# A recurrent layer's low-rank products, key norms and decays moved under its projections, 64-row logits and another order at the entrance

## The reference, cut to what matters

```python
# the indexer and the attention of layer 1
rel = relu(einsum('bthd,bsd->bths', qi_blk, ki)); score = einsum('bths,bth->bts', rel, wi_blk)
_, sel = lax.top_k(score, 64)
logits = einsum('btngd,btknd->btngk', qg, k_sel) * HEAD_DIM ** -0.5      # 64 numbers per head
# the recurrent layer
xx = token_shift(h) - h
xs = h[None] + xx[None] * mu[:, None, None, :]                            # six mixes
r, k, v = einsum('cbld,cde->cble', xs[:3], w_rkv)                         # three 1024x1024 projections
xw, xa, xg = xs[3], xs[4], xs[5]
w_log = -softplus(-(w0 + tanh(xw @ w1) @ w2)) - 0.5;  decay = exp(-exp(w_log))
a = sigmoid(a0 + (xa @ a1) @ a2)
g = sigmoid(xg @ g1) @ g2
kk = (k * k_k); kk = kk * rsqrt(max(sum(kk * kk, per head), 1e-24))
k = k * (1 + (a - 1) * k_a)
state = state * w_t + sa * b_t + v_t * k_t                                # b = kk * a, over 256 steps
y = state @ r_t
```

## Time and profile before

| | us |
|---|---|
| median of three runs | 1173.62 |
| profiled execution | 1176.45 |
| its span (first to last instruction) | 1174.8 |
| PE busy in the span | 1109.6 (94%) |
| DVE, ACT, POOL busy | 822.5, 639.3, 227.5 |
| mean granted PE clock | 0.967 of full speed |

### The profile page before, as it was taken

How to read it: one execution, slowest core, us unless ns; L and a number is a source line. 1 busy time by engine, 2 the same in 40 slices (tenths; PEclk the granted TensorE clock), 3 DMA queues, 4 the chain that set the end, 5 groups by cost and what they waited for, 6 DMA issues and landing times.

```text
span 1174.8 us, 23469 instructions
## 1 busy us (share of the span) xinstructions
PE 1109.6 (94%) x9384; PEld 997.0 (85%) x9384; DVE 822.5 (70%) x1103; ACT 639.3 (54%) x949; POOL 227.5 (19%) x171
## 2 busy tenths in 40 slices
PE   6889999999989999998699999989999999999887
PEld 5786798899879868998598899879997999998675
DVE  4687457767769669675767767775766877774774
ACT  4766356565646466324365565644534666664552
POOL 1000033344500005944023344510000000000000
PEclk9998999999999997999799999989999999999989
DMA  7522287877735520000467877746654655656200
GB/s 271 189 73 73 88 270 232 278 249 247 266 110 180 181 58 3 4 3 3 133 228 246 274 251 247 265 125 200 191 163 147 198 191 166 205 172 201 66 1 36
DMA packets 82138, 190.47 MB, mean 162 GB/s; under 512 B 5840, under 2 KB 6112, under 8 KB 81936
## 3 DMA queue, kind: packets, MB, share of 16 engines
q1 hardware_dynamic: 73184, 157.31, 41.4%
q0 software_dynamic: 7584, 27.53, 8.1%
q10 hardware_dynamic: 1296, 4.58, 1.0%
HBM read 188.34 MB, written 1.05 MB: 161 GB/s over the span
## 4 chain that ended last, share of the span: by engine, by line
PE 75%; DVE 11%; ACT 4%; DMA 4%; issue 3%; POOL 2%; ACTq 0%; DVEq 0%; POOLq 0%; SPq 0%
PE bank L1944 12%; PE bank L1945 12%; PE bank L1946 12%; PE bank L1920 4%; PE bank L1922 4%; PE bank L1921 4%; PE bank L2159 4%; PE bank L2160 4%; PE bank L2161 4%; PE bank L2335 3%; DVE w_lo L1185 2%; DMA mod_w<-in_w_mod_dram 2%; POOL mod_all L510 1%; PE bank L2231 1%; PE bank L2447 1%
## 5 line engine op out<-in xcount | busy, mean ns | idle before, releaser
L1185 DVE TENSOR_TENSOR w_lo<-raw,w_hi 128x1024 fp32r<-128x1024 f32 x296 | 390.4, 1338 | 211.4 <-ACT w_hi L652 211.2
L652 ACT ACTIVATE w_hi<-raw 128x1024 fp32r<-128x1024 f32 x296 | 310.2, 1056 | 296.9 <-PE bank L1946 149.3
L1944 PE MATMUL bank<-act_hi,w_hi 128*128 128x256 f32 x1392 | 390.2, 280 | 1.4 <-DVE act_lo L1227 0.8
L1945 PE MATMUL bank<-act_lo,w_hi 128*128 128x256 f32 x1392 | 390.1, 280 | 0.0
L1946 PE MATMUL bank<-act_hi,w_lo 128*128 128x256 f32 x1392 | 389.6, 280 | 0.0
L1944 PEld LDWEIGHTS bank<-act_hi,w_hi 128*128 128x128 f32 x1392 | 262.4, 189 | 4.2 <-issue 2.8
L1945 PEld LDWEIGHTS bank<-act_lo,w_hi 128*128 128x128 f32 x1392 | 262.3, 188 | 0.9 <-issue 0.2
L1946 PEld LDWEIGHTS bank<-act_hi,w_lo 128*128 128x128 f32 x1392 | 262.4, 188 | 0.0
L510 POOL TENSOR_TENSOR mod_all<-mod_all,mod_w 128x1024 f32<-128x1024 f32 x42 | 109.9, 2617 | 143.3 <-ACT mod_w L829 142.4
L2159 PE MATMUL bank<-w_hi,ff_hi 128*128 128x512 f32 x256 | 103.1, 403 | 8.2 <-DVE ff_lo L1424 8.2
L2160 PE MATMUL bank<-w_lo,ff_hi 128*128 128x512 f32 x256 | 103.3, 403 | 0.0
(11 more groups left out here) (315 smaller groups left out, 1484.2 us busy)
## 6 DMA issues: line engine op xcount, KB each, us to landing
raw<-in_mlp_w_up_dram SPq DMA_DIRECT2D x64, 512.0 KB, 4.9
raw<-in_mlp_w_down_dram SPq DMA_DIRECT2D x64, 512.0 KB, 4.4
raw<-in_dil_w_in_dram SPq DMA_DIRECT2D x64, 512.0 KB, 4.1
mod_w<-in_w_mod_dram POOLq DMA_DIRECT2D x48, 512.0 KB, 4.3
raw<-in_conv_w_in_dram SPq DMA_DIRECT2D x32, 512.0 KB, 4.3
raw<-in_rwkv_w_rkv_dram SPq DMA_DIRECT2D x24, 512.0 KB, 4.7
raw<-in_dsa_w_in_dram SPq DMA_DIRECT2D x16, 512.0 KB, 4.8
raw<-in_dsa_w_o_dram SPq DMA_DIRECT2D x8, 512.0 KB, 3.7
```

The source lines that it names most:

```text
L652: act.activation(w_hi[:, slot, :], raw[:, slot, :], ACT.Copy).then_inc(hi_ready, 1)
L1185: dve.tensor_tensor(w_lo[:, slot, :], raw[:, slot, :], w_hi[:, slot, :].bitcast(F32), ALU.subtract).then_inc(lo_ready, 1)
L1944: pe.matmul(dst, w_hi[:, slot, at], hi[:, kt, :], start=begin, stop=False, skip_group_check=True)
L1945: pe.matmul(dst, w_hi[:, slot, at], lo[:, kt, :], start=False, stop=False, skip_group_check=True)
```

## The change

Recurrent layer. The blocks come in the order keys, receptances, values. The mixes of decay and rate are made before block 2 into buffers of their own, and their first products run together after block 1, one in array columns 0 to 63 and the other in 64 to 127 of the same bank. The gate's first product, the head sums and half of the second products run after block 3, the other half after block 4. Roots are by one POOL instruction on 256 columns (`pow`) instead of ACT's square root, with its table loads, and DVE's reciprocal. Sigmoids, decay sums, exponentials and `ka` move between the splits of blocks 4 and 5. After the last block PE has `spread` and the gate's second product; the turned values move between the scan's first steps of u = 0 and u = 1. POOL makes its half of `k` and `b` only after both early operands. g2 is loaded after the gate's first product.

Layer 1. The indexer and attention logits use 64 array rows each, heads alternating between rows 0 to 63 and 64 to 127 and between two banks; `kiT`, the zeros of both and the copy on ACT are gone. The ReLU of the first four steps comes before `rope_bank(3, 2)`. ACT rounds the first activations after two granules, not four. The constants that layer 1 does not need, the norm row and the gate rows are loaded by ACT just before the attention units.

```diff
 # POOL
-            key_zeros()
-                pool.wait_ge(granule_used, STREAM["rwkv_out"])            # load_g2
+                pool.wait_ge(lora_full, 2)
             def rwkv():
                 load_g2()
+                pool.wait_ge(sums_ready, 1)
+                pool.tensor_tensor(per_head[:, :], per_head[:, :], half_neg[:, 0:1].broadcast_to([P, SEQ]), ALU.pow).then_inc(kk_inverse, 1)
+                pool.wait_ge(operands, 2)
                 pool.wait_ge(ka_ready, 2)
 # ACT, layer 1
-                split_block(base, 0)
+                for q in range(2): split_hi(base, q)
                 round_f(0)
+                for q in range(2, PER_BLOCK): split_hi(base, q)
...
-                for half in range(2): mv = act.activation(S["kiT"][rows, half, :], S["ki_rot"][rows, :], ACT.Copy)
                 split_block(base, 8)
+                for n in range(4): relu_scores(n)
                 act.wait_ge(granule_used, base + 8)
                 rope_bank(3, 2)
...
                 rope_bank(6, 6)
+                late_loads()                                              # five DMA issues
 # ACT, recurrent layer
+                splits(4, 8); leave(0); splits(8, 11); round_mix(1, (0, 1)); splits(11, 12); round_mix(1, (2, 3)); leave(1)
+                (tanh and copy of R["mid"] from bank[4])
+                splits(12, 13); round_mix(2, (0, 1)); splits(13, 14); round_mix(2, (2, 3)); splits(14, 16); leave(2)
+                splits(16, 18); (square of raw_kk); splits(18, 20); leave(3); (sigmoid of gmid)
+                open_gates(0); keep_a(0); splits(20, 24); leave(4)
+                open_gates(1); keep_a(1); decays(0); leave(5); decays(1)
 # DVE, recurrent layer
-                split_block(base, 4); mix(1); rest_mix(1); split_block(base, 8); mix(2); rest_mix(2); ...
+                splits(4, 6); mix_part(1, 0, 1); splits(6, 7); mix_part(1, 2, 3); splits(7, 8)
+                mix_part(2, 0, 1, 2, 3); mix_part(3, 0, 1); splits(8, 9); rest_part(1, 0); mix_part(3, 2); rest_part(1, 1)
+                splits(9, 10); mix_part(3, 3); rest_part(1, 2, 3); splits(10, 11); mix_part(4, 0, 1); splits(11, 12)
+                mix_part(4, 2, 3); splits(12, 13); rest_part(2, 0, 1, 2, 3); splits(13, 14); (raw_kk); splits(14, 15)
+                mix_part(5, 0, 1); splits(15, 16); mix_part(5, 2, 3); splits(16, 20)
+                dve.wait_ge(kk_sums, 1)
+                dve.tensor_scalar(per_head[:, :], bank[1][:, 0:SEQ], 1e-24, None, ALU.max).then_inc(sums_ready, 1)
+                sum_decays(0); splits(20, 22)
+                dve.tensor_tensor(R["k"][:, at, :], R["k"][:, at, :], R["ka"][:, at, :], ALU.mult).then_inc(k_early, 1)
+                splits(22, 24); sum_decays(1); means(0)
 # PE, recurrent layer, after block n
+                    if n == 1: lora_decay_and_rate()
-                        lora(0, ((0, LORA),))
+                    if n == 3: lora_gate(); head_sums(1, R["kk_square"]).then_inc(kk_sums, 1); second_lora(0)
-                        lora(1, ((0, LORA),))
+                    if n == 4: second_lora(1)
-                lora(2, ((0, GHALF), (GHALF, GHALF)))
 # PE, rwkv_mid
+                pe.wait_ge(kk_inverse, 1)
+                pe.wait_ge(lora2_ready, 8)
+                spread(4).then_inc(kk_spread, 1)
...
 # PE, scan_loop, first turn
                             pe.wait_ge(operands, u + 1)
-                            pe.wait_ge(*((vT_ready, 4) if u == 0 else (glora_ready, 4)))
+                            if u: turn_values()
+                            pe.wait_ge(*((glora_ready, 4) if u == 0 else (vT_ready, 4)))
 # PE, logits
+                    for e in range(2): (mask product into bank[2 * slot + e])
                     for j in range(2):
-                        mm = pe.matmul(dst, S["qT"][:, 2 * n + j, i * P:(i + 1) * P], S["kT"][:, n, :, 0:w], ...)
+                        for e in range(2):
+                            rows = slice(e * HD, (e + 1) * HD)
+                            mm = pe.matmul(bank[2 * slot + e][:, j * w:(j + 1) * w], S["qT"][rows, 2 * n + j, i * P:(i + 1) * P],
+                                           S["kT"][rows, n, 0:w], start=False, stop=True, skip_group_check=True)
```

More of the change, by code:

```diff
@@ L732, in dsa, with relu_scores @@
                 rope_bank(2, 1)
[L734 to L745, removed]
+                def relu_scores(n):
                     act.wait_ge(idx_full, n // 2 + 1)
@@ L898, in rwkv_in, with splits, keep_a @@
                     round_mix(0, (b,))
-                split_block(base, 4)
-                round_mix(1)
+                def splits(first, last):
+                    for k in range(first, last):
+                        split_hi(base, k)
+                def keep_a(half):
+                    act.wait_ge(less_ready, 1)
+                    act.wait_ge(kk_sums, 1)
+                    act.wait_ge(lora2_ready, 4 * half + 4)
+                    for pair in range(4 * half, 4 * half + 4):
+                        kept = act.activation(R["ka"][:, pair, :], mixer["a"][:, pair, :], ACT.Identity, bias=less_k_a[:, pair:pair + 1], scale=K_A[:, pair:pair + 1])
+                    kept.then_inc(ka_ready, 1)
@@ new lines, in open_gates @@
+                def open_gates(half):
+                    for pair in range(4 * half, 4 * half + 4):
+                        act.wait_ge(lora2_full, 2 * (pair // 2) + 2)
+                        src = slice(pair % 2 * SEQ, (pair % 2 + 1) * SEQ)
+                        for j, (bias, dst) in enumerate(((W0, less), (A0, mixer["a"]))):
+                            sg = act.activation(dst[:, pair, :], bank[4 + 2 * (pair % 4 // 2) + j][:, src], ACT.Sigmoid, bias=bias[:, pair:pair + 1])
+                        sg.then_inc(lora2_ready, 1)
@@ new lines, in second_lora @@
+                def second_lora(half):
+                    if half == 0:
+                        pe.wait_ge(mid_ready, 2)
+                    else:
+                        pe.wait_ge(lora2_ready, 4)
+                    for pair in range(4 * half, 4 * half + 4):
+                        for j, rows in enumerate((slice(0, LORA), slice(LORA, P))):
+                            mm = pe.matmul(bank[4 + 2 * (pair % 4 // 2) + j][:, pair % 2 * SEQ:(pair % 2 + 1) * SEQ], R["w2a2"][rows, pair * P:(pair + 1) * P],
+                                           R["mid"][rows, :], start=True, stop=True)
+                        mm.then_inc(lora2_full, 1)
@@ L2308, in rwkv_mid @@
                                 at = (j * CHUNKS + c) * CHUNK
-                                mm = pe.matmul(bank[b][rows, at:at + CHUNK], R["uv"][values, 2 * b + j, c, h, :], unit[values, :], start=True, stop=True)
+                                mm = pe.matmul(bank[4 + b][rows, at:at + CHUNK], R["uv"][values, 2 * b + j, c, h, :], unit[values, :], start=True, stop=True)
                     mm.then_inc(vT_full, 1)
```

398 lines of the change are left out of this document (220 added, 178 removed).

## The result

The changed kernel is slower: median 1181.25 us over 13 runs (1175.55 to 1186.01) against 1174.95 us of the kernel before, run beside it (1169.27 to 1179.35). The ratio is 1.0059, 95% interval 1.0041 to 1.0078. The forecast, 1168.7, named the wrong sign; its range, 1154 to 1188, holds the time. The profiled execution took 1179.7 us, with a span of 1178.0.

A forecast was written before the change was run, and what follows sets the result against it. PE, busy 94% of the span, was taken as the bound, with most time behind the recurrent layer's last block. 1176.45 - 11.7 + 11.6 - 4.8 = 1171.5 profiled, 2.83 above the median, so 1168.7; range 1154 to 1188.

The forecast's parts named there:

- the root: Recurrent layer: POOL's `pow` on 256 columns takes 19.4 us; 9.6 moves PE, plus 2 for lower clock, 11.6 lost.
- cover: Before the recurrent layer's last block: with DVE held, the root is hidden up to 9.8 us; each us above moves PE.
- (D): Recurrent layer: root long but DVE runs, PE idles 12 us at `spread`; time 1168 to 1177, near 1173; chance 0.11.
- (C): Recurrent layer, gap before block 5: DVE stands still, root 38 us; time 1187.6, range 1177 to 1191; chance 0.24.
- Up to the last block's end: Recurrent layer: 15.5 us of products inside the blocks for 7.3, so the last block ends 8.2 us later, at 433.2.
- DVE's pace: Recurrent layer, blocks 1 to 4: DVE's 35 us of work fits in 37; nothing charged, 3 us kept for the range.
- Behind the last block: Recurrent layer: first scan product at 442.0 instead of 460.4, u = 1 12.9 us earlier; gain 11.7, 8 to 13.
- The collision of POOL's products: Behind the last block: three DVE operands took 2.3 to 2.8 us beside POOL's products; POOL's added wait removes this.
- Layer 1: Attention units and block 12: halved logits gain 4.3 us, the block's end 0.5; gain 4.8 in all.
- or the clock drops: Layer 1's attention units: a case for the low end of their gain, 1 us of a range 1 to 5.
- Block 12: Layer 1: the block ends at 80.4 to 81.3 instead of 82.0, a gain of 0.5 us, 0 to 1.6.

The follow-up runs named there:

- root_act: The changed kernel with the root made by ACT (Sqrt) and DVE (reciprocal) in place of POOL's `pow`: 1162.18 us, ratio 0.9897 to the kernel before.
- rec_only: The kernel before with the recurrent part alone, the root on ACT and DVE, layer 1 as before: 1164.66 us, ratio 0.9905.
- after: The changed kernel itself, with POOL's `pow` and both parts of the change, against the kernel before: 1181.25 us, ratio 1.0059.
- l1_only: The kernel before with the layer-1 part alone, the recurrent layer as before: 1171.67 us, ratio 0.9965.
- the two halves: The kernel before with only the 64-row products and ReLU order, ratio 1.0005, or only the first splits' order and late loads, ratio 0.9991.

## Why the prediction was wrong, point by point

**The step that failed is the root**, in both of its halves. The term was 19.4 us and the row is 41.16; and the text charged it through DVE standing still, cover 9.8, where DVE ran and the cover was some 26 us (404.45 to the last block's end at 430.4). What happened is rival (D), which got 0.11: PE waits at `spread` until 445 (445.67), idle 12 us (15.2), the gate's second product at the lower clock (14.0), first scan product at 455 to 460 (462.5), u = 1 not before 464 (473.9). (D)'s price was too low. It said that the recurrent layer then gains nothing; in truth the layer loses 10.7 us (228.1 against 217.4). The root was 3.2 us longer than the 38 that (D) had, and the lower clock lasted to 468 and not only through the gate's product. The rest was in (D)'s own rows: from 445, `spread` and 13.6 us for the gate's product give 460 for the first scan product, and the 10 us from there to u = 1's end, which the forecast has (442.0 to 452.0), give 470 where the kernel before had 464.9. The range of 1154 to 1188 holds the time by luck: 1181.25 is above (D)'s own 1168 to 1177 and inside that of (C), in which DVE stands still, and it did not.

The root's size went wrong where I halved the slope of the earlier trace rows because "neither row is near 256 columns": the slope of two short rows, 0.148, was within 7% of the true 0.159, while the multiply's 2.3 ns a column, by which I tempered it, was of another operation and 70 times off.

**The sum, made again with what was measured** (recurrent terms from the traces): the recurrent part without the root -10.4 (207.0, the mean of the five profiles in which nothing of the root shows, against 217.4), the root +21.1 (228.1 - 207.0), layer 1 -4.1 by the timed runs (-2.0 by the traces). That is +6.6 to +8.7; the timed difference is +6.3, or 0.59% of 1175, 6.9. With the 0.9 us that `root_act` and `rec_only` leave to layer 1 it would be +9.8, so the sum closes to some 3 us and not better. By the timed runs alone the root is +19.0 (`after` less `root_act`) and all the rest together -12.1 (`root_act` less the kernel before).

**The root's 21.1** is 15.2 that stay when PE is kept busy (222.2 - 207.0, as long as PE's wait) and a lower clock of 5.9 behind it, where the prediction charged 9.6 and 2.

**Up to the last block's end: right.** From the layer's start to that end it is 85.6 us before and 94.3 after, 8.7 more; 8.2 were forecast. Decay and rate run side by side, sixteen matmuls at 64 columns in 3.7 us. No `w_lo` in blocks 2 and 3 made PE wait: DVE's pace held.

**Behind the last block: right in kind, a little too good.** With the root gone, the first scan product comes 10.9 us behind the last block (forecast 8.8), because ACT's exponentials and gate copies and the late values (0.71) come one after another; u = 1 ends 11.6 us earlier than before, measured from the layer's start, where 12.9 were forecast, and at the scan's end the gain is 10.4, forecast 11.7.

**The collision of POOL's products: half right.** The twelve operands start 0.60 to 0.70 us apart, as forecast. But the added wait did little for it: without it one operand is held, for 2.2 us, not three.

**Layer 1: right by one comparison, not shown in its parts.** Forecast 4.8 (1 to 5); `l1_only` gives 4.1 (2.5 to 5.9), `root_act` against `rec_only` 0.9, the two halves together 0.5. The shortened unit is there: 107.92 to 112.23 in the chain after, 4.31 us where it took 4.76, with 0.43 for the mask and 1.06 for the logits:

```profile
108.80 0.43 PE bank L2151 x2
109.23 1.06 PE bank L2155 x8
110.30 1.93 PE bank L2181 x16
112.23 0.88 PE bank L2167 x8
```

The logits' products go from 1.72 to 1.06 us and not to 0.86, and the values' product behind them from 1.73 (before) to 1.93, so a unit saves 0.45 us and not 0.86. The units up to 107 also run at half clock, where in the profile before the clock was back by 99.4 ("or the clock drops" stood in the range). Block 12 ends at 81.2, inside 80.4 to 81.3. The prediction did not have the 1.1 us at the layer's end, which are the clock's and stand in every profile with the 64-row products. The rest of the gain, and how large it is, stays open: neither half of the part gained alone.

## What to carry to other kernels

An instruction that moves to another engine must be priced on that engine at its full width, and when only its narrow rows are at hand, their slope is the estimate and a cheaper operation's slope is not. What decides is then its length less the cover: 21 us of root cost nothing here, 41 us cost 21 by the profiles, of which 6 were PE's lower clock after the idle wait. And single profiles can differ by 5 us in code that is the same (2.6 us at layer 1's end between two of one kernel); compare a stretch with the same stretch of several profiles before explaining it.

## What the runs showed of the hardware that was not expected

- POOL's `pow` costs 0.159 us a column of 128 partitions at every width seen (0.55, 0.70, 20.77 and 41.16 us for 1, 2, 128 and 256), 70 times its multiply (2.3 ns).
- For the 41.16 us of that `pow` DVE instructions with two SBUF inputs ran at their usual length, while 22 multiplies over 43.73 us made them 2.1 to 2.6 times as long (four decay sums 2.88 to 6.12 and 7.37, two `w_lo` 2.36 to 4.89) and were themselves stretched by little: 1.99 us each for 768 columns, where 2.36 for 1024 would give 1.77.
- Halving PE's work in a stretch at the lower clock did not bring its full gain: with the 64-row logits the granted clock came back at 100 to 108.5 (ten profiles), without them at 99 to 102.5 (four). At the layer's end the clock fell to 0.50 in the four and stayed at 1.00 in the ten, 1.1 us of the chain.
